# Token lists of all experts made once per layer, and routing weights carried in the gathered rows, in a two-layer DeltaNet/MLA mixture-of-experts trunk

## The reference, cut to what matters

```python
def route(xf, w_router, bias):
    scores = jax.nn.sigmoid((xf @ w_router).astype(F32))
    biased = scores + bias.astype(F32)
    ...
    _, idx = lax.top_k(jnp.where(expert_mask, biased, -jnp.inf), TOP_K)
    w = jnp.take_along_axis(scores, idx, axis=-1)
    w = w / (w.sum(-1, keepdims=True) + 1e-20) * ROUTED_SCALE
    return idx, w
...
    def step(acc, inp):
        tok, wt, e = inp
        y = swiglu(x_pad[tok], w_gate[e], w_up[e], w_down[e]).astype(F32) * wt[:, None]
        return acc.at[tok].add(y), None
```

## Time and profile before

| | us |
|---|---|
| median of 3 runs (lowest, highest) | 2580.89 (2578.11, 2583.52) |
| the profiled execution's own time | 2584.4 |
| its span in the trace | 2582.7 |
| PE busy | 2317.7 (90%) |
| DVE busy | 1811.2 (70%) |
| ACT busy | 1357.8 (53%) |
| POOL busy | 825.4 (32%) |

### The profile page before, as it was taken

One profiled execution on the slowest core, in us unless ns is written; L12 is line 12 of the kernel. 1 busy time (PEld: TensorE's weight loads), 2 busy tenths in 40 slices (PEclk: granted clock), 3 DMA queues, 4 the chain that ended last, 5 costly groups with the idle time before them and its releaser, 6 DMA issues. The chain is left out here.

```text
span 2582.7 us, 39490 instructions
## 1 busy us (share of the span) xinstructions
PE 2317.7 (90%) x11685; PEld 1862.2 (72%) x11685; DVE 1811.2 (70%) x2757; ACT 1357.8 (53%) x2066; POOL 825.4 (32%) x467
## 2 busy tenths in 40 slices
PE   8989788878979999999999399998799999999992
PEld 6867777667668888888887265576588888888872
DVE  3759555545269999999997222433589999999993
ACT  3332211220258777777777122312377777888882
POOL 0000332210025555555555000000145555555551
PEclk9999899989789999999999599797899999999996
DMA  5321000000279999999998411013599999999993
GB/s 182 98 66 53 1 1 1 1 18 33 102 268 338 339 346 346 342 341 343 343 346 261 160 41 49 1 37 115 181 337 349 349 353 343 348 341 346 336 326 96
DMA packets 174997, 534.46 MB, mean 207 GB/s; under 512 B 23009, under 2 KB 52673, under 8 KB 174657
## 3 DMA queue, kind: packets, MB, share of 16 engines
q1 hardware_dynamic: 148720, 461.82, 49.2%
q0 software_dynamic: 23456, 67.14, 11.3%
q10 hardware_dynamic: 2736, 4.38, 0.5%
HBM read 495.31 MB, written 50.14 MB: 211 GB/s over the span
## 5 line engine op out<-in xcount | busy, mean ns | idle before, releaser
L1206 DVE TENSOR_TENSOR gu_l<-ring,gu_h 128x1024 fp32r<-128x1024 f32 x512 | 728.8, 1461 | 17.3 <-ACT gu_h L1107 6.3
L1107 ACT CAST gu_h<-ring 128x1024 fp32r<-128x1024 f32 x512 | 518.8, 1077 | 15.8 <-DVE y L1223 9.7
L1329 POOL TENSOR_TENSOR down_l<-ring,down_h 128x1024 fp32r<-128x1024 f32 x130 | 316.2, 2432 | 488.3 <-ACT down_h L1115 485.0
L1045 PE MATMUL bank<-gu_h,xgT_l 128*128 128x512 f32 x1024 | 411.8, 402 | 0.0
L1115 ACT CAST down_h<-ring 128x1024 fp32r<-128x1024 f32 x260 | 259.5, 1046 | 284.3 <-PE bank L1076 276.9
L1047 PE MATMUL bank<-gu_h,xgT_h 128*128 128x512 f32 x1024 | 400.8, 391 | 0.0
L1046 PE MATMUL bank<-gu_l,xgT_h 128*128 128x512 f32 x1024 | 399.8, 390 | 0.0
L1339 POOL DMA_INDIRECT xg<-h_rows,list_idx x128 | 142.6, 1114 | 705.4 <-issue 485.9
L1351 POOL DMA_INDIRECT moe_sum<-y,out_idx x128 | 272.7, 2130 | 66.4 <-issue 66.4
L1074 PE MATMUL bank<-down_h,hmT_l 128*128 128x512 f32 x544 | 231.6, 426 | 19.8 <-POOL down_l L1329 19.8
L1047 PEld LDWEIGHTS bank<-gu_h,xgT_h 128*128 128x128 f32 x1024 | 192.4, 188 | 42.4
(11 more groups left out here) (292 smaller groups left out, 3867.1 us busy)
## 6 DMA issues: line engine op xcount, KB each, us to landing
ring<-in_moe_w_gate SPq DMA_DIRECT2D x256, 512.0 KB
ring<-in_moe_w_up SPq DMA_DIRECT2D x256, 512.0 KB
ring<-in_moe_w_down SPq DMA_DIRECT2D x256, 512.0 KB
ring<-in_a_w_in SPq DMA_DIRECT2D x32, 512.0 KB
ring<-in_a_w_out SPq DMA_DIRECT2D x8, 512.0 KB
h_rows<-y SPq DMA_DIRECT2D x8, 512.0 KB, 2.6
moe_sum<-y ACTq DMA_DIRECT2D x8, 512.0 KB, 5.2
resid<-moe_sum SPq DMA_DIRECT2D x8, 512.0 KB, 6.2
```

The costliest lines, as they stand in the source:

```text
L1045: nc.tensor.matmul(out, lhsT=xl, rhs=wh, start=k == 0, stop=False)
L1107: nc.scalar.copy(gu_h[:, c, :, :], gate_up_cols(gate_slot, c * CH // 2, CH // 2)).then_inc(gu_hi.sem, 1)
L1206: nc.vector.tensor_tensor(gu_l[:, c, :, :], gate_up_cols(gate_slot, c * CH // 2, CH // 2), gu_h[:, c, :, :].bitcast(F32), ALU.subtract).th ...
L1329: nc.gpsimd.tensor_tensor(down_l[:, 1, :], ring[:, down_slot, CH:2 * CH], down_h[:, 1, :].bitcast(F32), ALU.subtract).then_inc(down_lo.sem, 1)
```

## The change

The lists of all experts are made once in the shared stage. DVE writes for every token and expert a number that is larger for an earlier token, or zero if the token isn't routed there (`token_at`); PE turns this so that a partition is an expert in one half of the sequence (`pe_tokens_T`); eight rounds of top-8 and replace on DVE take the 64 largest of each row in order (`dve_extract`); PE turns them back (`pe_slots`), and one DVE operation gives `index_all`, an expert's list in each column. The two halves of the sequence alternate in a list, and an expert's count is now twice the larger half (`pe_counts`, `dve_counts`). A step has no one-hot comparison, no list product and no copies of lists. Instead POOL itself copies the expert's column ahead of each gather and each scatter. Rows in `h_rows` grow from 1024 to 1088 numbers: the last 64 are the token's routing weights for all experts, stored once by ACT, and DVE picks one column of the gathered rows for an expert (`dve_slot_w`). POOL's wait for the shared results moves from ahead of step 0 to its first scatter. ACT casts expert 0's first weights one token tile earlier. In the attention part some semaphores are shared with the DeltaNet part.

```diff
-        h_rows = nc.dram_tensor("h_rows", (T, D), F32).ap()
+        h_rows = nc.dram_tensor("h_rows", (T, D + E), F32).ap()
...
+            def pe_tokens_T(pe):
+                pe.wait_ge(token_done.sem, token_done.base + 1)
+                for j in range(2):
+                    last = nc.tensor.transpose(bank[5][:, j * P:(j + 1) * P], token_at[:, j, :, :].rearrange("p h e -> p (h e)"), ident)
+                last.then_inc(token_T.sem, 1)
+            def pe_slots(pe, lists_wait, done):
+                lists_wait(pe)
+                for h in range(2):
+                    last = nc.tensor.matmul(bank[5][:, T // 2:T // 2 + E], lhsT=spread[:, :, :].rearrange("p s h -> p (s h)"), rhs=const[:, C_ID, h * E:(h + 1) * E], start=h == 0, stop=h == 1)
+                last.then_inc(done.sem, 1)
...
                 pe_gate_up(pe, r, i)
-                if not last or r + 3 < E:
-                    pe_gather_list(pe, r + 3, i)
...
+            def dve_slot_w(v, r, i):
+                g = gathered[r % 2]
+                v.wait_ge(g.sem, g.base + 16 * (r // 2 + 1) + 32 * i)
+                if r >= 4:
+                    v.wait_ge(y_done.sem, y_done.base + r - 3 + 4 * i)
+                nc.vector.tensor_copy(slot_w[:, r % 4:r % 4 + 1], xg[r % 2][:, bass.ds(D + r + 4 * i, 1)]).then_inc(slot_w_done.sem, 1)
+            def dve_extract(v, first, rounds, own):
+                for n in range(first, first + rounds):
+                    own(nc.vector.max(lists[:, 8 * n:8 * n + 8], remaining[:, n % 2, :]))
+                    own(nc.vector.match_replace(out=remaining[:, (n + 1) % 2, :], in_to_replace=lists[:, 8 * n:8 * n + 8], in_values=remaining[:, n % 2, :], imm_value=0.0))
...
             def dve_step(v, r, i, last=False):
-                if not last or r + 3 < E:
-                    dve_onehot(v, r + 3, i)
                 if r >= 1:
                     dve_down_lo(v, r - 1, i)
                 if not last or r + 1 < E:
+                    dve_slot_w(v, r + 1, i)
                     dve_rows_T(v, r + 1, i)
...
-                if r >= 1:
-                    dve_out_list(v, r - 1, i)
-                if not last or r + 3 < E:
-                    dve_list(v, r + 3, i)
...
             def pool_gather(pool, r, i):
-                pool.wait_ge(list_copied.sem, list_copied.base + r + 1 + 4 * i)
-                bump(pool)
                 if r >= 2:
                     pool.wait_ge(xgT_ready.sem, xgT_ready.base + 2 * r - 2 + 8 * i)
                     bump(pool)
+                    pool.wait_ge(slot_w_done.sem, slot_w_done.base + r - 1 + 4 * i)
+                    bump(pool)
+                    pool.wait_ge(gathered[r % 2].sem, gathered[r % 2].base + 16 * (r // 2) + 32 * i)
+                    bump(pool)
+                nc.gpsimd.tensor_copy(gather_idx[:, r % 2:r % 2 + 1], index_all[:, bass.ds(r + 4 * i, 1)]).then_inc(gather_idx_done.sem, 1)
+                pool.wait_ge(gather_idx_done.sem, gather_idx_done.base + r + 1 + 4 * i)
+                bump(pool)
...
                     for tt in range(TT):
                         act_silu(act, tt, 0, True)
+                        if tt == 1:
+                            act.wait_ge(w_done.sem, w_done.base + 1)
+                            act.dma_start(h_rows[:, D:D + E].rearrange("(t p) e -> p t e", p=P), slot_weight[:, :, :]).then_inc(w_stored.sem, 16)
                         act_hm_T(act, tt, 0, True)
+                        if tt == 1:
+                            act_gu_hi(act, 0, 0, range(CH_GU))
                         if tt >= 1:
                             act_store_sum(act, tt - 1)
-                        if tt == 2:
-                            act_gu_hi(act, 0, 0, range(CH_GU))
...
                     for r in range(3):
                         pool_gather(pool, r, 0)
-                    for c in sum_stored:
-                        pool.wait_ge(c.sem, c.base + 32)
-                        bump(pool)
                     steps(pool, pool_step)
```

More of the change, by code:

```diff
@@ L959, in moe @@
             w_sum = sb(f"w_sum_{layer}", [P, TT], scope=mo)
-            entry = sb(f"entry_{layer}", [P, TT, E, 2], scope=mo)
-            rank = sb(f"rank_{layer}", [P, TT, E], scope=mo)
+            slot_weight = sb(f"slot_weight_{layer}", [P, TT, E], scope=mo)
+            token_at = sb(f"token_at_{layer}", [P, 2, 2, E], scope=mo)
+            remaining = sb(f"remaining_{layer}", [P, 2, T // 2], scope=mo)
+            lists = sb(f"lists_{layer}", [P, SLOTS], scope=mo)
+            spread = sb(f"spread_{layer}", [P, SLOTS, 2], scope=mo)
+            counts2 = sb(f"counts2_{layer}", [P, 2, E], scope=mo)
             most = sb(f"most_{layer}", [P, 1], scope=mo)
@@ L1348, in pool_scatter @@
                     bump(pool)
+                if r == 0:
+                    for c in sum_stored:
+                        pool.wait_ge(c.sem, c.base + 32)
+                        bump(pool)
+                nc.gpsimd.tensor_copy(out_idx[:, r % 2:r % 2 + 1], index_all[:, bass.ds(r + 4 * i, 1)]).then_inc(out_idx_done.sem, 1)
+                pool.wait_ge(out_idx_done.sem, out_idx_done.base + r + 1 + 4 * i)
+                bump(pool)
                 def move(n):
@@ L1532, in moe @@
                 ov = {name: sem(f"over_{name}") for name in (
-                    "onehot", "list", "index", "gathered", "rowsT", "rowsT_copied", "gate_up", "silu", "product", "hmT", "hmT_copied", "down", "result", "added")}
+                    "own", "lists", "slots", "index", "column", "gathered", "slot_w", "rowsT", "rowsT_copied", "gate_up", "silu", "product", "hmT", "hmT_copied", "down", "result", "added")}
             else:
-                ov = {"onehot": onehot_done, "list": list_ready, "index": list_copied, "gathered": gathered0, "rowsT": xgT_ready, "rowsT_copied": xgT_copied,
+                ov = {"own": sel_done, "lists": lists_done, "slots": slots_ready, "index": index_done, "column": gather_idx_done, "gathered": gathered0, "slot_w": slot_w_done, "rowsT": xgT_ready, "rowsT_copied": xgT_copied,
                       "gate_up": gu_ready, "silu": silu2_done, "product": hm_done, "hmT": hmT_ready, "hmT_copied": hmT_copied, "down": down_ready,
@@ L1582, in expert @@
                     def expert(n, e):
-                        passes = n // E + 1
-                        pe.wait_ge(ov["onehot"].sem, ov["onehot"].base + n + 1 + e)
-                        for tt in range(TT):
-                            last = nc.tensor.matmul(bank[5][:, 0:2], lhsT=onehot[:, 0, tt, :], rhs=entry[:, tt, bass.ds(e, 1), :].rearrange("p e c -> p (e c)"), start=tt == 0, stop=tt == TT - 1)
-                        last.then_inc(ov["list"].sem, 1)
                         pe.wait_ge(ov["gathered"].sem, ov["gathered"].base + 16 * (n + 1) + 16 * e)
@@ L1596, in expert @@
                         last.then_inc(ov["gate_up"].sem, 1)
-                        pe.wait_ge(ov["product"].sem, ov["product"].base + n + 1 + passes + e)
+                        pe.wait_ge(ov["product"].sem, ov["product"].base + n + 1 + e)
                         for j in range(2):
@@ L1606, in expert @@
                         last.then_inc(ov["down"].sem, 1)
-                    over_passes(pe, lambda: None, expert)
+                    over_passes(pe, lambda p: pe_slots(pe, lambda pe: pe.wait_ge(ov["lists"].sem, ov["lists"].base + p), ov["slots"]), expert)
                 @block.scalar
```

225 lines of the change are left out of this document (110 added, 115 removed).

## The result

The changed kernel takes **2651.8 us** (median of 4 runs, 2646.3 to 2653.6) against 2582.2 for the kernel before in the same measurement: 1.0268 times as long (95% interval 1.0247 to 1.0289). Forecast were 2545 us and a range from 2508 to 2578, so the sign was wrong. The profiled execution's span went from 2582.7 to 2651.9 us, +69.2.

A forecast was written before the change was run, and what follows sets the result against it. DMA was taken to bound the steady step, with the compute chain level with it. Terms of -7 (steady), -25.4 (layer starts) and -3 us (layer end) sum to -35.4, giving 2545 us from the median 2580.9, range 2508 to 2578.

The forecast's parts named there:

- the sum for POOL: Steady step: POOL's two copies with hops, gather, low part of down and scatter take 9.8 us, under 10.6.
- Rival D: Each gather and scatter: POOL becomes the bound; at 2.9 us per copy with hop, step 11.8, 2691 us; 9%.
- Rival A: Steady step: DMA is the wall, the forecast itself, 2545 us; 60%.
- The steady term: Steady step limited by DMA, wider rows included: -0.06 us over 61 steps in two layers, -7 us.
- The start: Layer start: DMA's saturated phase begins 12.7 us earlier per layer, 8.3 + 4.4 (shorter shared stage); -25.4 us.
- the moved wait: Layer start: POOL's wait for shared stores moves to its first scatter, freeing the slot 8.3 us earlier per layer.
- The layer end's -3: End of layer 1: ACT's casts trail the loads by about 3 us; a DMA-bound layer has no such trail.
- B: Steady step: no wall, DMA takes in what compute asks for; step 9.8 or 9.6 us, 2450 us; 12%.
- C: Layer start: another wait holds POOL or PE in step 0, so the 8.3 us stay; 2562 us; 8%.
- E: Gathered rows: the wider row is dear, an extra packet each at 0.2 us; 2637 us; 6%.
- F: Steady step: PE waits 1 us, its clock is granted lower, PE needs 11.5 us; 2655 us; 3%.
- The terms for DVE: Shared stage: eight rounds on DVE, 0.4 us for top-8 and 0.5 for replacing with its load, 8 in all.

The follow-up runs named there:

- dve_both: Changed kernel with both one-column index copies, for gather and scatter, made by DVE a step ahead instead of by POOL; 2542.4 us, 0.9862 of the kernel before.
- b_wide: Kernel before with rows of 1088 instead of 1024 elements stored and gathered, the added columns unused; 2585.0 us, 1.0008 of the kernel before.
- b_start: Kernel before with only POOL's wait for the shared stores moved from ahead of step 0 to its first scatter; 2562.0 us, 0.9938 of the kernel before.
- dve_out: Changed kernel with only the scatter's index copy moved from POOL to DVE; 2564.4 us, 0.9931 of the kernel before.
- pool_ahead: Changed kernel with both copies still on POOL, made one expert ahead, behind down's low part; 2546.2 us, 0.9856 of the kernel before.
- b_pool: Kernel before with only two one-column copies added on POOL, ahead of gather and scatter, each waited for; 2691.6 us, 1.0414 of the kernel before.
- out_first: Changed kernel with the scatter's copy and its wait put ahead of the waits for the result and the last scatter's landing; 2560.7 us, 0.9906 of the kernel before.
- dve_gather: Changed kernel with only the gather's index copy moved from POOL to DVE; 2601.0 us, 1.0075 of the kernel before.
- count_first: Changed kernel with POOL reading the expert's count ahead of each copy instead of behind the wait for it; 2558.5 us, 0.9903 of the kernel before.
- wait_inside: Changed kernel with the wait for each copy put inside the branch, right ahead of its DMA; 2559.1 us, 0.9908 of the kernel before.
- copy_more: Changed kernel with a third one-column copy on POOL, waited for, behind the gather's copy; 2669.7 us, 1.0345 of the kernel before.

## Why the prediction was wrong

**The failed step** is the sum for POOL: "2 x (0.15 + 1.73) + 1.40 + 2.42 + 2.23 = 9.8 us". Its terms were fair: the copy is 0.18 alone and 0.7 to 0.8 in its place, the hop 1.5 to 1.6, gather, low part and scatter 1.2, 2.45 and 2.0; with them the sum is 10.3, or 9.8 less the copy's overlap, the figure forecast. What was left out is the wait for the last scatter's landing, 1.7 us a step: in the code it stood ahead of the new copy, and in the profile before it left no row, as the landing was over when POOL came. The floor of the step isn't POOL's sum but the ring of the landings: 7.3 us from the end of an issue to the landing, 2.3 for the copy and what stands behind it, 2.0 for the issue, 11.55 in all. Before, POOL had 4.6 us idle ahead of each gather (the 4.75 of the earlier trace rows is one), and landing, reading of the count and branches all lay in it or beside work. The change added to the ring, per step, two copies (1.5), the queue's work ahead of the gather in line (1.6) and more of it ahead of the scatter (1.2), and uncovered the landing (1.7): 6.0, less the overlap of 0.45, against 4.6. What is over, 0.9 us, is what the step grew by. (This is the same idle time booked on POOL, not a second cause.)

**Rival D** had the place, the sign and nearly the size (a step of 11.8, 2691 us), and 9 in 100. Its mechanism was only half right: it needed 2.9 us for a copy with its hop, and they took 2.3 (0.75 + 1.55), at which D itself has POOL just at 10.6. The rest is the landing, which D has no term for either.

**Rival A, DMA as the wall**, is right for the kernel without this fault: dve_both stands at 2542.4 beside 2545. But it gets there by other parts. The steady term (-7) is wrong in sign: the 53 steps to the last expert took 5.6 and 4.5 us *more* per layer than before, with rows 6% wider (b_wide: +0.08 a step). The start was worth 18.2 and 18.3 us a layer, not 12.7: of it 7.3 and 7.8 are the moved wait (8.3 forecast, b_start). The rest is some 10.7 against 4.4 forecast; 5.5 of it show between the first and the fourth product of the shared stage (36.7 us before, 31.2 in dve_both), and how the remainder divides was not tested. Another 17 us came from between the layers (below). The layer end's -3 didn't show. So 2542 beside 2545 is luck: errors of opposite sign met.

**B** (no wall) falls: 10.75 us at a share of 1.01, and less only with fewer bytes. **C** falls, the start gain was there. **E** falls, a row is one packet (b_wide). **F** falls as the cause: the clock was 0.97 to 0.98 in the changed kernel's steady windows, and dve_out has 0.98 in both with a step of 10.89; in dve_both, with PE waiting too, it is 0.99.

**The terms for DVE** held: in the shared stage of the changed kernel MAX8 takes 0.43 and MATCH_REPLACE8 with its load 0.50 us (0.4 and 0.5 forecast).

Shown by undoing: that the copies' place on POOL makes the loss (dve_both, pool_ahead, b_pool), that the landing ahead of the scatter's copy is part of it (out_first, dve_gather), and that the count's reading behind the copy's wait is another (count_first, wait_inside). Both work through one threshold: either brings the step near DMA's 10.7 us (10.8 to 11.0), so their shares don't add up. That the ring of the landings sets the changed kernel's step is read from the traces; no run changed the landing alone.

## What to carry to other kernels

When small work is put on an engine that issues DMAs, walk once round that engine's whole ring with every wait in it, those too that the old profile shows as free: they were free only at the old spacing. Put what needs no data (reading a count, branching, an index copy) ahead of a wait, never behind it; here the order alone was worth 91 to 93 us of 2652. A chain from a DMA's landing to its own next issue is a bound by itself (11.55 us here), even where the engine in it has time to spare.

The copies on DVE, or a stage ahead on POOL, make the version to take: 0.986 of the kernel before.

## What the runs showed of the hardware

**A queue that waits for its own engine costs what it could have done ahead.** A small copy is 0.18 us by itself (pool_ahead), and the next copy can start 0.2 us behind it (copy_more). An indirect DMA starts 1.5 us behind it if the count is read in between, 0.9 if it is read ahead (wait_inside), and 0.5 behind POOL's last instruction if it waits for no copy of POOL's (dve_both, 22.5 us in 47 waits).

**DVE and POOL together.** DVE's low part of gate and up, the same instruction, took 1.66 us in the changed kernel's window and 1.22 in dve_both's:

```profile
L1220 DVE TENSOR_TENSOR gu_l<-ring,gu_h 128x1024 fp32r<-128x1024 f32 x174 | 282.8, 1660 | 8.1 <-ACT gu_h L1119 3.4
```

```profile
L1231 DVE TENSOR_TENSOR gu_l<-ring,gu_h 128x1024 fp32r<-128x1024 f32 x185 | 221.7, 1221 | 60.0 <-ACT gu_h L1119 58.8
```

The mean hides two kinds. Of the 173 that start in 900:1400 of the changed kernel, the 118 that lie beside no low part of POOL took 1.21 us (at most 1.23), the 55 that do took 2.62. The timeline shows it: POOL's low part runs from 1012.45 to 1014.90, and three of DVE's beside it take 5.65 us, the next one alone 1.21.

```profile
1010.33 5.65 DVE L1220 TENSOR_TENSOR gu_l<-ring,gu_h 128x1024 fp32r<-128x1024 f32 x3
...
1016.35 1.21 DVE L1220 TENSOR_TENSOR gu_l<-ring,gu_h 128x1024 fp32r<-128x1024 f32 x1
```

The Trainium skill (SBUF — State Buffer, Who interferes with whom) says that a DVE instruction with two SBUF inputs contends with a GpSimd instruction that reads SBUF. The traces agree: DVE's low part of the rows (`xgT_l`), one of whose inputs is in PSUM, took 0.69 us beside POOL's low part and away from it. In dve_both POOL's low part comes elsewhere in the step, and in 900:1340 none of DVE's for gate and up lies beside it. This isn't what bounded the step: in layer 1 count_first had the slow kind (1.66 in the mean) and wait_inside hardly any (1.23), with 10.71 and 10.72 us a step over the 53 steps.

**PE's clock between the layers.** For 30 us, some 210 us behind layer 0's last product, PE is busy without a gap in every kernel, but the granted clock differs. Windows at that place, of the kernel before and of dve_both:

```profile
1622.00:1652.00 30.00, 30.00 (x86) 17.41 (x85) 12.17 (x48) 8.97 (x37) 0.00 (x0) 0.54 0.00 1
```

```profile
1610.00:1640.00 30.00, 30.00 (x149) 17.75 (x149) 18.85 (x67) 14.51 (x54) 0.00 (x0) 1.00 0.00 1
```

86 against 149 matmuls in 30 us of full activity: mostly at 1.2 GHz in one, at 2.4 in the other, 0.85 in the changed kernel. The stretch from the last product of layer 0 to the first of layer 1 took 387.5 us before at a mean clock of 0.82, 375.7 changed (0.85), 370.3 in dve_both (0.87) and 380.3 in pool_ahead. The change itself touches semaphores in that stretch, but b_start, which doesn't, had 376.6 us at 0.85. Why the clock comes back sooner in one than in another is open; no experiment held it fixed, and 10 to 17 us of any difference between two profiled executions here may be this.
